# The query product of two memory attentions, from f32 matmuls to three fp32r matmuls each

## The reference, cut to what matters

```python
def memory_xattn(h, mem_h, wq, wk, wv, wo):
    q = (h @ wq).reshape(b, s, XA_HEADS, XA_HEAD_DIM)      # h: 512 x 1024, wq: 1024 x 1024
    k = (mem_h @ wk).reshape(b, m, XA_HEADS, XA_HEAD_DIM)  # mem_h: 256 x 1024
    v = (mem_h @ wv).reshape(b, m, XA_HEADS, XA_HEAD_DIM)
    ...
for l in range(DEPTH):     # DEPTH = 2
    ...
    x = x + memory_xattn(rmsnorm(x, xa_ln[l]), rmsnorm(mem, xa_mem_ln[l]),
                         xa_wq[l], xa_wk[l], xa_wv[l], xa_wo[l])
    x = x + squared_relu_mlp(rmsnorm(x, ff_ln[l]), ff_w1[l], ff_w2[l])
```

## Time and profile before

| | us |
|---|---|
| median of 3 runs | 4385.27 |
| lowest and highest | 4384.09, 4387.93 |
| profiled execution | 4397.9 |
| its span | 4396.1 |
| TensorE busy | 4003.5 |
| DVE busy | 1538.6 |
| ACT busy | 1155.9 |

### The profile page before, as it was taken

One profiled execution on the slowest core, in us unless ns is written; L12 is line 12 of the kernel. 1 busy time (PEld: TensorE's weight loads), 2 busy tenths in 40 slices (PEclk: granted clock), 3 DMA queues, 4 the chain that ended last, 5 costly groups with the idle time before them and its releaser, 6 DMA issues. The chain is left out here.

```text
span 4396.1 us, 43429 instructions
## 1 busy us (share of the span) xinstructions
PE 4003.5 (91%) x17234; PEld 2842.6 (65%) x17234; DVE 1538.6 (35%) x2479; ACT 1155.9 (26%) x1972; POOL 107.0 (2%) x228
## 2 busy tenths in 40 slices
PE   7879798999999999989989999799998888887999
PEld 3447556878557885668765545688887333665777
DVE  2343304333102342243342431444334145544443
ACT  1122303222213442232240110321123322543222
POOL 0032000000000000000000000000000001000000
PEclk9879899999987999999999999899999876998999
DMA  3335321222210002212221101111123100001212
GB/s 127 134 115 194 123 96 58 76 96 96 108 58 1 1 3 84 80 73 98 94 102 39 66 19 39 39 57 57 50 94 135 53 0 1 1 20 58 95 67 96
DMA packets 29914, 307.93 MB, mean 70 GB/s; under 512 B 3715, under 2 KB 5348, under 8 KB 9029
## 3 DMA queue, kind: packets, MB, share of 16 engines
q1 hardware_dynamic: 29766, 305.88, 18.9%
HBM read 303.77 MB, written 2.10 MB: 70 GB/s over the span
## 5 line engine op out<-in xcount | busy, mean ns | idle before, releaser
L295 PE MATMUL psum<-h_all,ring 128*128 128x256 f32 (+3 forms) x2688 | 871.5, 484 | 30.0 <-DVE h_all L686 9.1
L295 PEld LDWEIGHTS psum<-h_all,ring 128*128 128x128 f32 (+2 forms) x2688 | 508.2, 189 | 386.2 <-issue 340.6
L523 PE MATMUL psum<-operand_rounded,weights_rest 128*128 128x512 f32 (+1 forms) x1360 | 521.3, 383 | 62.3 <-DVE operand_rest L494 62.3
L299 PE MATMUL psum<-operand_rounded,weights_rest 128*128 128x512 f32 x1216 | 490.0, 403 | 80.3 <-DVE weights_rest L318 80.3
L524 PE MATMUL psum<-operand_rounded,weights_rounded 128*128 128x512 f32 (+1 forms) x1360 | 518.2, 381 | 0.0
L525 PE MATMUL psum<-operand_rest,weights_rounded 128*128 128x512 f32 (+1 forms) x1360 | 517.7, 381 | 0.0
L301 PE MATMUL psum<-operand_rest,weights_rounded 128*128 128x512 f32 x1216 | 479.0, 394 | 0.0
L300 PE MATMUL psum<-operand_rounded,weights_rounded 128*128 128x512 f32 x1216 | 479.0, 394 | 0.0
L492 DVE TENSOR_TENSOR weights_rest<-ring,weights_rounded 128x1024 fp32r<-128x1024 f32 x170 | 208.1, 1224 | 575.4 <-ACT operand_rounded L476 575.4
L475 ACT ACTIVATE weights_rounded<-ring 128x1024 fp32r<-128x1024 f32 x170 | 179.9, 1058 | 633.1 <-PE psum L525 568.5
L523 PEld LDWEIGHTS psum<-operand_rounded,weights_rest 128*128 128x128 f32 x1360 | 261.7, 192 | 114.9 <-issue 55.7
(11 more groups left out here) (335 smaller groups left out, 4353.9 us busy)
## 6 DMA issues: line engine op xcount, KB each, us to landing
ring<-in_ff_w SPq DMA_DIRECT2D x32, 2048.0 KB, 7.7
ring<-in_w_mod SPq DMA_DIRECT2D x24, 2048.0 KB, 7.9
ring<-in_ffn_up SPq DMA_DIRECT2D x22, 2048.0 KB, 7.8
ring<-in_ffn_down SPq DMA_DIRECT2D x33, 1024.0 KB, 4.8
ring<-in_a_w_in SPq DMA_DIRECT2D x4, 2048.0 KB, 7.9
ring<-in_xa_wq SPq DMA_DIRECT2D x4, 2048.0 KB, 7.8
ring<-in_xa_wk SPq DMA_DIRECT2D x4, 2048.0 KB, 7.9
ring<-in_xa_wv SPq DMA_DIRECT2D x4, 2048.0 KB, 7.8
```

The costliest lines, as they stand in the source:

```text
L295: mm = nc.tensor.matmul(out, lhs, rhs, start=(t == 0), stop=(t == kt - 1))
L299: nc.tensor.matmul(out, rest, top_in, start=(t == 0), stop=False)
L523: nc.tensor.matmul(k.bank(m, n), rest, top_in, start=first, stop=False)
```

## The change

The attention layer moves into the small arena, with the memory norm's scratch region placed at 13400 in place of 20000, buffers for the two parts are placed before the query product and given back behind it, and the product gets `parts`. Key and value products stay as they are.

```diff
 def cross_attention_layer(k, l, norm, following):
 
+    k.change_arena(SMALL_ARENA)
+    parts_scope, parts = k.place_parts()
     mem = k.region(0, KT, MEM)
     Q, K, V = k.region(2048, KT, SEQ), k.region(6144, KT, MEM), k.region(8192, 2, D)
     k.load_later([(mem, k.dram["mem"])], "memory_landed")
-    norm.placed_later(20000)
+    norm.placed_later(13400)
     drained = k.counter("bank_drained")
     tokens = lambda t, s, n: k.h[:, t, s:s + n]
-    product(k, "xa_wq", tokens, [(0, SEQ)], scalar=copy_out(k, lambda c, m, g: Q[:, 4 * c + m, :]), norm=norm)
+    product(k, "xa_wq", tokens, [(0, SEQ)], scalar=copy_out(k, lambda c, m, g: Q[:, 4 * c + m, :]), norm=norm, parts=parts)
+    parts_scope.close()
     product(k, "xa_wk", tokens, [(SEQ, MEM)], scalar=copy_out(k, lambda c, m, g: K[:, 4 * c + m, :]))
```

## The result

| | before | after |
|---|---|---|
| median of 7 executions each, us | 4387.93 | 4401.93 |
| lowest, highest | 4384.09, 4396.30 | 4398.14, 4405.21 |
| profiled span | 4396.1 | 4403.4 |

The ratio of after to before is 1.0030, with a 95% interval of 1.0018 to 1.0042: slower by 0.3%, some 13 us. The forecast was 4392.3 us in a range of 4386 to 4399, with 0.31 on slower. Ten further executions of the same kernel gave 4398.79, a ratio of 1.0021 (1.0012 to 1.0031). So the sign is clear, and the size lies near 11 us.

What follows compares the result with a forecast made beforehand. TensorE, busy 4003.5 of 4396.1 us, was taken as the bound. Per layer, start 5.6 + 7.2 = 12.8 us later less 9.3 saved gives +3.5; two layers +7.0 on 4385.3 make 4392.3 us, range 4386 to 4399.

Steps and rivals of the forecast that it cites:

- The level to which the sum was added: Timed median of the kernel before, 4385.3 us, 12.6 us below its profiled execution; that difference was carried over unchanged.
- the sums: TensorE's sums for the memory norm before the query product: idle longer beforehand, costed at nothing, 0.4 us either way.
- the cold start: Query product starts at half clock after about 7 us idle: 2.1 us lost a layer, range 1.6 to 2.8.
- The product's gain: Split query product on TensorE: eight banks 5.44 us apart instead of 6.87, 11.4 us a layer at full clock.
- The 13.7 us: Query product's gain a layer if three passes replaced four, forecasting 4387.6 us; set aside for the trace's rows.
- ACT's roundings ahead of the squares: ACT rounds eight token tiles before table load and memory squares, making the memory's chain 5.6 us later a layer.
- rival C: ACT loses another 1.29 us a layer between last rounding and first square: +9.6 us, 4394.9; chance 0.16.
- DVE's order: DVE cuts the first weight tile only after scaling the memory: query product starts 7.2 us later a layer.
- Rival A: TensorE's clock does not fall in the 7 us idle before the query product: 4388.1 us; chance 0.07.
- the rest of the edit: Small arena and scratch at 13400 move addresses; DVE gets one more register instruction per feed-forward tile; no cost added.
- Rival B: Memory's chain overlapped, query product starting 11.6 us after first scaling: -8.5 us a layer, 4368 us; chance 0.07.

Runs made afterwards that it cites:

- weights_first: The changed kernel, but ACT rounds and DVE cuts the first two weight tiles ahead of the memory's logarithm and scaling; 4382.34 us, ratio 0.9984 to before.
- filled: The changed kernel plus 15 unread f32 matmul pairs on TensorE between the memory's sums and the query product; 4398.25 us, ratio 1.0021 to before.
- interleaved: The changed kernel with ACT's memory squares set between roundings, and DVE cutting two weight tiles before the memory's scaling; 4370.0 us, ratio 0.9956 to before.

## Why the prediction was wrong

Two things failed. The level to which the sum was added was 4.8 us too low: a median of three executions, with "2 us for a median of runs" allowed for it. Without that the time would lie inside the range. And the sum was too small by a quarter, in two of its terms: the sums "at nothing", and the 2.1 us of the cold start. The mechanism, the two queues and the slow start, stood. By its steps, per layer:

1. The product's gain, 11.4 us: right. Banks are 5.44 us apart (7 x 5.44 = 38.08 = 610.23 - 572.15), and two kernels that differ in the product and 0.2 us of start are 11.4 us apart. One f32 matmul takes as long as 3.8 of the fp32r ones (6.87 / 8 = 0.859 against 5.44 / 24 = 0.227 us). The 13.7 us that the prediction drew from the four passes of "FP8 and Floating Point Precision" of the Trainium skill (TensorE Precision Notes) are not there.
2. ACT's roundings ahead of the squares, +5.6: right, 5.63 and 5.60. Its 1.29 us from load to square held, so rival C is out: nothing more than the load is lost between rounding and square (548.62 to 549.91). The drain that "ScalarE: Activation LUTs" of the Trainium skill ("What ACT_TABLE_LOAD costs") puts beside the load, for a switch to a different set, does not show here: neither the load behind a rounding nor the square behind the load has a gap. This load follows a logarithm and an exponential of the same set with only roundings between, so it may be no switch; but two loads of the kernel after that stand 1.53 us apart (461.19 and 462.72), with one activation between them, show no gap either.
3. The sums, at nothing with 0.4 either way: wrong. From first square to logarithm it is 6.93 and 6.99 us, where it was 6.22 and 6.58: +0.7 and +0.4. The text said that TensorE "will be idle longer" before them and drew nothing from it; the granted clock over the sums was 0.57 in both layers, where it had been 0.63 and 0.59. The low level lasted 5.5 and 5.6 us from the first sum, where it had lasted 4.1 and 4.8. The bound of 0.4 was the difference between two layers whose sums both start some 5.2 us after the first scaling, with 9 us of idle time before them; now they start at 10.8 behind 14.65 us. Whether the longer idle time or the later place does it was not tested.
4. DVE's order, +7.2: right to 0.2 (start 6.80 us after the logarithm, 7.03 forecast, since cut to matmul is 1.31 and not 1.46 us). weights_first took 7.3 us of start away by undoing it.
5. The cold clock, 2.1 us: mis-sized. First bank out after 8.51 and 8.56 us, 7.73 forecast; 2.9 us lost against 5.64, and 2.7 to 2.8 against the measured warm start of filled. The range of 1.6 to 2.8 had been read from restarts; the longest of them was read short, from a window that ends after 5.5 us, while that start (1621.86) stayed at the low level for 5.8 us. The price that was taken is that of one start, the feed-forward stage's in layer one, which had 4.0 us at the low level. The product here had matmuls 0.43 us apart for about 5.9 us (563.64 to 569.5). The idle time does not tell which it will be: 6.60 us were followed by 5.8 us at the low level, 6.84 by 5.9, 15.41 by 4.0 before the change and 15.40 by 5.2 after it, 19.79 by 5.6 and by 2.8 in two executions of one kernel. So a single start is one draw, and the one that was copied was a short one. Rival A, no fall of the clock, is out: 0.50 over the first 5.9 us.

Sum: 5.6 + 0.7 + 7.0 - 8.5 = +4.8 and, in layer two, +4.5, for +3.5 forecast: 9.3 us in place of 7.0. Outside the stages another 2 us or so are lost, which no step had; the prediction gave "the rest of the edit" no cost.

The larger miss is the reference. The step "the timed median is 12.6 us below the profiled execution, and I carry the difference over unchanged" took the distance of one execution from three others for a property of profiling. It was the spread of the executions. On the kernel's own level, 4390.1 us over 67 executions, the forecast 7.0 us would have given 4397, and the 9.3 us of the stages 4399.4; the kernel after has a median of 4400.1 over its 17. So of the 9.6 us of the miss 4.8 are the level and 2.3 the terms; the 2.5 that are left are the rest of the span and the draw of the seven executions, and the runs do not separate these two. That the profiled span of after (4403.4) met the forecast (4403.1) is no confirmation: the two profiled executions lay 8.1 and 4.5 us above the mean span of their kernels; the agreement is luck.

Rival B was wrong for this kernel and right as a statement on what it left lying: with the memory's chain overlapped it gave a start of 11.6 us after the first scaling and 4368 us. The interleaved kernel starts at 11.44 and takes 4370.0.

The chances: 0.31 on slower, from a sum put just below the bound of 0.2%. With 2.8 us for the cold start and the 0.4 us of the sums, both inside its own ranges, the sum is 7.0 + 2 x (0.7 + 0.4) = 9.2 us and lies beyond that bound of 8.8.

## What to carry to other kernels

A product that gets cheaper on TensorE by work on ACT and DVE is worth what its start still has: write down both queues ahead of its first matmul, and put every instruction that the first matmul does not need behind the ones that it does. Here the same edit costs 11 us with the helpers' work queued block by block, and saves 20 us with the same instructions interleaved. And a profiled execution is one of many: subtract stage times inside the traces, but add the difference to the median of many executions, and do not read a distance between one profile and three timed runs as a constant. Price a start of TensorE from several starts and take their spread: the start behind 19.79 us of idle time ran slow for 2.8 us in one execution and for 5.6 in another, which by half of it is an estimated 1.4 and 2.8 us.

## What the runs showed of the hardware that was not expected

- The span of an execution of this one-core kernel goes with TensorE's mean granted clock: over 60 executions of the kernel before, 4392.5 us at 0.935 and 4382.8 at 0.938. Its two profiles show restarts whose slow stretch is longer in one execution than in the other (5.6 and 2.8 us behind the same 19.79 us of idle time); that the other executions differ by the same is not shown.
- The length of the idle time before a start did not set how long it ran slow: the feed-forward start, always behind 15.4 us, ran slow for 4.0 and 4.4 us in the two layers of the kernel before and for 5.2 us in both of the kernel after.
- Matmuls of the split product are 0.43 us apart at the low clock and 0.23 at the high one; a start after 6.84 us of idle time, behind sums that had run at a mean clock of 0.57, kept the low one for about 5.9 us, and cost 2.7 to 2.8 us against a start kept warm by 15 otherwise useless matmuls. Those matmuls gave back 2.7 to 2.8 us a layer in the stage, and 1 to 2 us in all in the time, if anything.
- On ACT the step from rounding to table load and from load to squares cost nothing beyond the load's own 1.28 us, whether ACT had idled before it or not.
